# The last expert unit's rows kept in SBUF and added by one-hot matmuls; the other rows read back from DRAM beside its work

## The reference

```python
x = x + g1 * out                                        # the mixer
h = rms_norm(x, P['norm_ffn'][l]) * (1 + sc2) + sh2
x = x + g2 * hier_moe(h, P, l)                          # top 2 of 32 experts, each silu(h Wg) * (h Wu) Wd
...
y_sample = rms_norm(x, norm_final)
```

## Time and profile before

| what | us |
|---|---|
| median of 3 runs (1552.59 to 1553.79) | 1553.10 |
| profiled execution, its own time | 1553.09 |
| its span, first to last instruction | 1551.1 |
| PE busy in the span | 1339.0 (86%) |
| DVE busy | 524.7 (34%) |
| ACT busy | 338.8 (22%) |
| POOL busy | 116.0 (7%) |
| mean granted PE clock | 0.932 of 2.4 GHz |

### The profile page before, as it was taken

How to read it: one execution, slowest core, us unless ns; L and a number is a source line. 1 busy time by engine, 2 the same in 40 slices (tenths; PEclk the granted TensorE clock), 3 DMA queues, 4 the chain that set the end, 5 groups by cost and what they waited for, 6 DMA issues and landing times.

```text
span 1551.1 us, 17020 instructions
## 1 busy us (share of the span) xinstructions
PE 1339.0 (86%) x6480; PEld 819.6 (53%) x6480; DVE 524.7 (34%) x1076; ACT 338.8 (22%) x722; POOL 116.0 (7%) x140
## 2 busy tenths in 40 slices
PE   5999888999997998886999997978869979988864
PEld 2554675466883333332465557878868833323322
DVE  3010563333232111011557817578761421110104
ACT  2100314233231111110326213221231211111111
POOL 2400010000001111110000010000000011111100
PEclk8999898999999999899999998999887999999998
DMA  9952576065446999994532200000025469999942
GB/s 349 311 187 72 200 191 250 32 260 207 190 156 241 399 409 418 418 418 194 192 129 89 82 0 1 28 1 1 1 105 208 161 245 405 412 418 418 418 173 115
DMA packets 81301, 329.79 MB, mean 213 GB/s; under 512 B 18791, under 2 KB 19985, under 8 KB 56512
## 3 DMA queue, kind: packets, MB, share of 16 engines
q1 hardware_dynamic: 66224, 300.54, 49.8%
q0 software_dynamic: 14992, 28.10, 5.7%
HBM read 321.09 MB, written 30.58 MB: 227 GB/s over the span
## 4 chain that ended last, share of the span: by engine, by line
PE 59%; DMA 18%; DVE 14%; issue 6%; ACT 2%; SPq 0%; POOL 0%; DVEq 0%; ACTq 0%; POOLq 0%
PE psum L906 19%; PE psum L1230 11%; PE psum L998 9%; DMA ring<-in_moe_w_up 6%; DMA arena<-in_moe_w_up 5%; PE psum L1256 3%; DMA wide<-in_moe_w_up 3%; PE psum L930 3%; PE psum L878 2%; PE psum L993 2%; DVE arena L2300 1%; DVE wide L2260 1%; DMA ring<-in_ada_w 1%; DMA arena<-h_rows,slot_token 1%; PE psum L937 1%
## 5 line engine op out<-in xcount | busy, mean ns | idle before, releaser
L906 PE MATMUL psum<-wide,ring 128*128 128x384 f32 x704 | 239.9, 501 | 2.9 <-ACT wide L1526 1.9
L906 PEld LDWEIGHTS psum<-wide,ring 128*128 128x128 f32 x704 | 165.3, 238 | 70.0 <-issue 8.1
L1230 PE MATMUL psum<-arena 128*64 128x512 f32 x480 | 151.6, 621 | 25.5 <-DMA ring<-in_moe_w_up 13.1
L1230 PE MATMUL psum<-ring,arena 128*64 128x512 f32 x384 | 138.9, 635 | 13.7 <-DMA wide<-in_moe_w_up 8.2
L998 PE MATMUL psum<-ring 128*128 128x128 f32 x872 | 116.2, 292 | 17.5 <-issue 8.3
L998 PEld LDWEIGHTS psum<-ring 128*128 128x128 f32 x872 | 110.2, 205 | 22.9 <-issue 13.1
L2180 DVE TENSOR_TENSOR arena<-arena,psum 128x256 f32<-128x256 f32 x34 | 14.3, 421 | 307.3 <-ACT arena L1669 307.3
L906 PE MATMUL psum<-ring,wide 128*128 128x512 f32 (+2 forms) x336 | 116.1, 507 | 0.0
L1230 PEld LDWEIGHTS psum<-arena 128*64 128x64 f32 x480 | 48.0, 143 | 102.9 <-issue 100.1
L878 PE MATMUL psum<-cst 128*128 128x128 f32 (+1 forms) x298 | 84.7, 435 | 13.6 <-issue 10.7
L1230 PE MATMUL psum<-wide,arena 128*64 128x512 f32 x224 | 90.5, 622 | 6.7 <-DMA arena<-in_moe_w_up 6.7
(11 more groups left out here) (491 smaller groups left out, 1691.2 us busy)
## 6 DMA issues: line engine op xcount, KB each, us to landing
ring<-in_ada_w SPq DMA_DIRECT2D x24, 2048.0 KB, 11.0
arena<-in_moe_w_gate SPq DMA_DIRECT2D x28, 1024.0 KB, 14.5
arena<-in_moe_w_up SPq DMA_DIRECT2D x28, 1024.0 KB, 21.9
arena<-in_moe_w_down SPq DMA_DIRECT2D x28, 1024.0 KB, 22.7
ring<-in_moe_w_gate SPq DMA_DIRECT2D x24, 1024.0 KB, 14.2
ring<-in_moe_w_up SPq DMA_DIRECT2D x24, 1024.0 KB, 18.6
ring<-in_moe_w_down SPq DMA_DIRECT2D x24, 1024.0 KB, 20.7
ring<-in_w_in_odd SPq DMA_DIRECT2D x7, 2048.0 KB, 8.1
```

The source lines that it names most:

```text
L906: ins = mm(out, lhs(k), rhs(k), start=(k == 0), stop=(k == n - 1))
L1230: ins = mm(psum[half, 2 + s, :].rearrange("p (w f) -> p w f", w=2), hg[s][:, k, half], buffers[UNITS[q][h] % BUFFERS][0][:, :, k, :], star ...
```

## The change

For each layer:

- Unit 16 is not scattered any more. Its rows stay in `yrow[0]`. The count of scatters on each semaphore is adapted (`scatters`).
- SP waits for the scatters of units 14 and 15 and then loads `ysel`. `ysel` moves from `arena` into the first one and a half slots of `ring`, since `arena` is in use by unit 16.
- DVE builds `hot_last`, 128 slots x 384 tokens, one where the slot's token is that token and zero elsewhere: three comparisons of 128 x 128, put ahead of unit 16's other work, and one small addition in the router, which keeps the unit's tokens in `spares[:, 7:8]`. Slots without a token have a row of zeros.
- DVE's three additions of `ysel` stand inside unit 16, between its `act_s` copy and the scaling of columns 512 to 1023 (`yb`). They stood behind the branch.
- On PE each `yt` bank is now a sum of four matmuls: columns m of `yrow[0]` with `hot_last` (128 x 384), and for each token tile the columns of `ysel[0]` with the identity (128 x 128). The 15 `keep_busy` matmuls are gone.
- Of the odd layer's weights SP loads the first (`load(n_even)`, slot 2 of `ring`) without waiting for `chosen2_in`; the second and later ones wait until the last `yt` bank is computed, since slots 0 and 1 hold `ysel`.
- Three semaphores of the even layer become one (`even_norms`, counts 1, 2, 3).

The diff (line numbers of the changed kernel are up to 3 lower before DVE's part and 9 higher after it):

```diff
         def scatters(l, n):
-            return (PAIRS + 1 - n % 2) // 2 * l + n // 2 + 1
+            return (PAIRS - 1) // 2 * l + n // 2 + 1
...
-        used[0] = base + 3 * 2 * T
-        used[0] = max(used[0], work_end)
-        ysel = [carve(TILES * D).rearrange("p (c d) -> p c d", c=TILES)]
-        used[0] = base + 3 * 2 * T
-        ysel.append(carve(TILES * D).rearrange("p (c d) -> p c d", c=TILES))
+        ysel = [ring_words[:, n * TILES * D:(n + 1) * TILES * D].rearrange("p (c d) -> p c d", c=TILES) for n in range(2)]
+        hot_last = hg[1].rearrange("p k s -> p (k s)")[:, 0:T]
...
-                for n in range(PAIRS - 2, PAIRS):
+                for n in range(PAIRS - 3, PAIRS - 1):
                     sp.wait_ge(S(f"gathered_scattered{n % 2}"), 16 * scatters(l, n))
...
             moe(0)
-            sp.wait_ge(S(f"chosen{TILES - 1}_in"), 32)
-            for n in range(n_even, len(weights)):
+            load(n_even)
+            sp.wait_ge(*computed("yt", 0, KD - 1))
+            for n in range(n_even + 1, len(weights)):
                 load(n)
...
-                        scatter(n)
+                        if n < PAIRS - 1:
+                            scatter(n)
...
                     if m == 0:
-                        keep_busy(b, 10)
-                        pe.wait_ge(S("chosen0_in"), 32 * (l + 1))
-                        keep_busy(b, 5)
+                        pe.wait_ge(S("hot_last"), l + 1)
+                    mm(b[:, 0:T], yrow[(PAIRS - 1) % 2][:, m::KD], hot_last, start=True, stop=False)
+                    if m == 0:
                         pe.wait_ge(S("chosen_added"), TILES * (l + 1))
                     for c in range(TILES):
-                        ins = nc.tensor.transpose(b[:, tok(c)], ysel[0][:, c, m::KD], ident)
+                        ins = mm(b[:, tok(c)], ysel[0][:, c, m::KD], ident, start=False, stop=(c == TILES - 1))
                     ready(ins)
...
+                o_(ts(spares[:, 7:8], bank("ix", l)[:, PAIRS - 1:PAIRS], float(NOWHERE), None, ALU.add))
...
             def gathered(l):
                 kind = "gathered_"
                 for q in range(PAIRS):
+                    if q == PAIRS - 1:
+                        dve.wait_ge(S(f"{kind}gu_computed"), PAIRS * l + q)
+                        for c in range(TILES):
+                            ins = ts(hot_last[:, c * P:(c + 1) * P], iota, float(P * c), spares[:, 7:8], ALU.add, ALU.is_equal)
+                        ins.then_inc(S("hot_last"), 1)
...
+                    if q == PAIRS - 1:
+                        for c in range(TILES):
+                            dve.wait_ge(S(f"chosen{c}_in"), 32 * (l + 1))
+                            done(tt(ysel[0][:, c, :], ysel[0][:, c, :], ysel[1][:, c, :], ALU.add), "chosen_added")
                     dve.wait_ge(S(f"{kind}y1_computed"), PAIRS * l + q + 1)
...
-                for c in range(TILES):
-                    dve.wait_ge(S(f"chosen{c}_in"), 32 * (l + 1))
-                    done(tt(ysel[0][:, c, :], ysel[0][:, c, :], ysel[1][:, c, :], ALU.add), "chosen_added")
```

More of the change, by code:

```diff
@@ L808, in _ @@
                                mst[0:1, 0, :, :].rearrange("p d h -> p (d h)")).then_inc(S("ml_out"), 16)
-                pool.wait_ge(S("kv_norm"), 1)
+                pool.wait_ge(S("even_norms"), 1)
                 pool.dma_start(o["kv"][0, 0], ckn[:, 0, :]).then_inc(S("even_out"), 16)
@@ L1043, in _ @@
             beside("cqT", 0)
-            pe.wait_ge(S("mla_norm"), 1)
+            pe.wait_ge(S("even_norms"), 2)
             for k in range(3):
@@ L1063, in _ @@
             beside("hmT", 0)
-            pe.wait_ge(S("hm"), 1)
+            pe.wait_ge(S("even_norms"), 3)
             for h in range(4):
@@ L1960, in _ @@
                         ins = stt(ckn[:, c], tail[:, c, CKV0:CKV0 + KV_RANK], ms6[:, c:c + 1], gkv, ALU.mult, ALU.mult)
-                    done(ins, "kv_norm")
+                    done(ins, "even_norms")
                     for c in range(TILES):
                         ins = stt(cqn[:, c], tail[:, c, CQ0:CQ0 + Q_RANK], ms3[:, c:c + 1], gq, ALU.mult, ALU.mult)
-                    done(ins, "mla_norm")
+                    done(ins, "even_norms")
                     dve.wait_ge(*taken("oN", 2))
@@ L1990, in _ @@
                               ALU.mult, ALU.mult)
-            done(ins, "hm")
+            done(ins, "even_norms")
             beside("cqT", 0)
```

## The result

The changed kernel takes 1566.26 us (median of 6 runs, 1562.91 to 1571.10), the kernel before 1554.59 (6 runs, 1552.59 to 1561.87): a ratio of 1.0073, 95% interval 1.0047 to 1.0100. It is slower by about 12 us. The forecast, 1553.3 with a range up to 1557.0, is wrong.

The account below looks back on a forecast made before the run. It took the serial chain around both combinations as the bound: PE late by branch and fillers, then DVE's pace. Layer 0's +0.9 and layer 1's -0.7 gave +0.2 us on 1553.09, so 1553.3, range 1549.5 to 1557.0.

Parts of the forecast that it names:

- Loads earlier: Before both combinations: loads follow unit 15's scatter, third addition starts at 733.8 and 1508.7, loads hidden only in part.
- The collision: Layer 0: loads or PE's branch run into the 2 MB of weights, up to 5 us slower, 1558.3; chance 0.17.
- Additions ahead of `yb`, branch behind it: Before both combinations: `yb` comes at 735.8 and 1510.7, PE's branch follows, combination starts at 740.3 and 1515.3.
- The combination is dearer on PE: Both combinations: a group costs 1.38 us on PE, eight cost 11.0, against 6.2 of DVE before; PE sets the pace.
- The clock: Start of both combinations: PE, idle beforehand, restarts at 1.2 GHz and loses 2.35 us, bounds 1.6 and 2.8.
- What is late next: Behind the combinations: layer 0's norm matmuls end at 759.0, root 0.9 us later; layer 1's final squares 0.7 earlier.
- The sum: Whole kernel: +0.9 - 0.7 = +0.2 us over the two layers, 1553.3 against the profiled 1553.09.
- DVE's pace: Both combinations: the four matmuls overlap so far that DVE keeps the pace, 14 us faster, 1539; chance 0.03.
- short branch: PE's branch before both combinations costs what it costs SP, 7.1 us less in all, 1546.2; chance 0.04.
- low clock throughout: Both combinations: clock stays low, groups take 22.0 us instead of 13.35, norm another 5.4, 1576; chance 0.07.
- no overlap: Loads start only after PE's end of unit 16, both layers 7 us later, 1567.6; chance 0.02.
- over 17 us: Both combinations: sign that the prediction is wrong, groups taking over 17 us (or under 9), where 13 were expected.

Follow-up runs that it names:

- the run with `yb` first: Changed kernel with the three additions moved behind the scaling of unit 16's second half on VectorE: 1555.91 us; with tiles also turned by transposes, 1546.27 us.
- The pauses: Kernel before, with layer 0's combination delayed by 5 more filling matmuls (1562.78 us) or by 5 VectorE operations that change nothing (1559.97 us).

## Why the prediction was wrong

*Loads earlier: right.* Scatter to first load 7.2 and 5.0 us (7.1 and 5.3 forecast); first load to the start of the third addition 10.4 and 10.5 us (12.05 and 11.04). The 2 MB of weights issued behind them did them no harm. The collision, which had 0.17 of the chances, shows at most in PE's wait at the branch, 0.8 us longer here and nearly 3 once `yb` came first. The odd layer's later weights were hidden, as worked out: its projection took 69.58 us in both kernels.

*Additions ahead of `yb`, branch behind it: right.* PE began 5.3 and 4.5 us behind the scaling, 4.48 and 4.60 forecast, and its own branch lasted 4.1 and 3.6 us. By the rule of the Trainium skill that the prediction cited ("Runtime: NRT & Kernel Launch", "Instruction fetch mechanics") the stall is paid again; the trace agrees. So do the four variants whose branch was short in layer 1, if the target was at hand there; that it was is not shown. What I listed as a fact of the change, `yb` behind the additions, was also its second fault, and the places of the run with `yb` first show that 3 to 6 us were to be had there.

*The combination is dearer on PE: this is the step that failed.* It read "One group m costs 0.67 + 3 x 0.24 = 1.38 us", from the earlier trace rows. Those rows have the shape and type of the new matmuls, but their stationary operands lie side by side. The new ones step by 8 words, each weight load takes 0.14 us more, and a 128-column matmul takes two loads. A group measured 2.07 us, 16.5 for eight, where 1.38 and 11.0 were forecast. The old transposes stepped just as far and took 0.12 each, which hid the cost. With the step taken out, the sum holds: 1.31 us a group, 13.5 and 12.1 us for the combination with its cold start (13.35 forecast), marks at +0.0 and -2.0 (+0.9 and -0.7), and a time 1.7 us under the kernel before. The forecast was of that kernel, not of this one.

*The clock: the right way, too large.* Eight groups at full clock are 16.5 us; they took 17.3 to 17.9, so the cold start cost 0.8 to 1.4 us, where I took 2.35, with 1.6 as the lower bound. With neighbouring columns it cost 3.0 and 1.6. The first group, at half clock, took 2.8 us for 2.07: the strided loads are as long at either level (312 to 339 ns in all), so only the rest gets slower.

*What is late next: right.* The norm's matmuls lay wholly behind the groups, and the root came 5.4 us behind them; the final squares came 3.1 us behind the first transposes, as worked out.

*The sum.* With 17.3 and 17.6 us for 13.35, +0.2 becomes +8.4: 1561.5. That is 8.4 of the 12 measured. The table has only +4.0 for this profile, since PE began 7.7 and 9.8 us behind unit 16 where the forecast had 11.4 and 10.4; in layer 0 unit 16 ran 2.8 us long at a low clock, while the loads went on. The other 3 to 4 us of the time, and the twice as large effect of layer 0, stay open. The pauses rule out that every delay there doubles; they leave a part that may depend on what PE does, and I have no run that shows it.

*The rivals.* "DVE's pace", "short branch", "low clock throughout" and "no overlap" did not happen in the changed kernel. The short branch, given 0.04, did happen in layer 1 of four of its relatives. The 21 us of low clock that the earlier trace rows brought for "low clock" don't tell transposes from other work: they hold 5.6 us of transposes, 5.1 of idle time, 6.8 of narrow matmuls and the first 3.4 of a projection. None of the rivals named the group's price in the upward direction, though the text itself gave "over 17 us" for the groups as the sign of a wrong prediction, and 17.3 came. The range had no term for it: the only bound that I had put on the matmul was for the clock.

## What to carry to other kernels

When a matmul takes the place of a transpose, or a price is taken from another row of the same shape, compare the access pattern of the stationary operand too: at PE's full clock float32 weights read 8 words apart cost 0.33 us a load for 0.19, and a narrow matmul has little to hide it. If data must be picked with a step, let the transpose do it, and add what remains by one matmul onto the transposed bank; or write the operand in the right order on an engine that waits anyway. And where an engine stops at a branch behind a semaphore, give that semaphore before the work that the branch can cover.

## What the runs showed of the hardware

- A float32 weight load of 128 x 128 with a step of 8 words takes 0.312 to 0.340 us at either level of PE's clock; with neighbouring words 0.19 at the full and 0.33 at the half. So at half clock the step is nearly free (a group 2.69 to 2.81 us with it, 2.56 to 2.69 without). That the reading of the operand sets it at the full clock is argued from this, not shown; steps other than 1 and 8 were not tried.
- Transposes with the same step load in 0.19 us at the full clock, 0.23 at the half, and have one load, not two. Which of their operands is loaded the rows don't say.
- VectorE writing 1024 float32 per partition with a step of 128 words took 1.90 us for 1.23, ScalarE 512 in 1.16 for 0.69.
- PE's branch over the flag had three lengths in the thirty places of the fifteen profiles: 3.3 to 4.1 us in 23 of them, 6.1 us in three, 0.35 us in four. The three long ones are layer 0 of the kernels with `yb` first, where the DMA share beside it was 0.90 to 0.95, against 0.5 at most beside the others. The four short ones are all in layer 1, of the four kernels that have transposes and no fillers. What makes it short is not shown; no run varied it alone. Where `yb` was what PE waited for, PE began 4.3 to 5.3 us behind it with a branch of the middle length, 7.2 to 7.3 with a long one, and 1.3 with the short one.
- In four of fifteen profiles PE's clock fell to the half level in a stretch (279 to 287) of untouched code, for 5 to 6 us of lateness up to the experts. One profile of a kernel of 1.5 ms can be off by that much, and only distances between near marks should be read from it.
